# Two routers, a tail and one block's dense part put in a new order, in a kernel of three layers on one core

## The reference

```python
x = x + concat([mla_out, rw_out]) @ w_o
t = rms_norm(x, g_ffn)                       # block 1
group_logits = t @ w_group + b_group         # 4 groups, the best one is taken
expert_logits = t @ w_expert + b_expert      # 8 experts in it, the best two
weights = softmax(top_vals) * group_probs[gsel]
x = x + sum_e combine[:, e] * ((silu(t @ w_gate[e]) * (t @ w_up[e])) @ w_down[e])

for i in (0, 1):                             # block 2
    mix = concat([pool(x @ w_in), conv(x @ w_in)]) @ w_out[i]
    x = layer_norm(ALPHA * x + mix, ln1_g[i], ln1_b[i])
    f = swiglu(x) if i == 0 else moe_swiglu(x, router_w)   # 2816 wide; 8 experts, 3584 wide, best two
    x = layer_norm(ALPHA * x + f, ln2_g[i], ln2_b[i])
    x = x + sigmoid(x @ ple_gate_w[i]) * (p[i] @ ple_w[i])
```

## Time and profile before

| what | value |
|---|---|
| time, median of 3 runs | 1973.67 us (1969.62 to 1973.97) |
| the profiled execution | 1974.57 us |
| its span in the trace | 1972.8 us |
| TensorE busy | 1765.5 us (89%) |
| VectorE busy | 452.2 us (23%) |
| ScalarE busy | 197.6 us (10%) |
| read from memory | 543.5 MB, 276 GB/s over the span |
| granted clock of TensorE, mean | 0.956 of full speed |

### The profile page before, as it was taken

The page is one execution under the profiler, slowest core; times in us unless marked ns, Lnnn a source line. Parts: engine busy times, 40 slices in busy tenths (PEclk is TensorE's granted clock), DMA queues, the critical chain, the costliest instruction groups (busy, mean ns, idle before and its releaser), DMA issues.

```text
span 1972.8 us, 21931 instructions
## 1 busy us (share of the span) xinstructions
PE 1765.5 (89%) x9504; PEld 946.2 (48%) x9504; DVE 452.2 (23%) x771; ACT 197.6 (10%) x333; POOL 41.2 (2%) x123
## 2 busy tenths in 40 slices
PE   7888867677698999989989999999989999998778
PEld 6676654443484444455755434444444434432233
DVE  2664631121273000022832011011011011010003
ACT  2241111111102000001120000000000000000001
POOL 4001000000000000000000000000000000000000
PEclk9889869998899999999988999999999999999999
DMA  7022238999926234353417999979999999999991
GB/s 260 3 86 87 103 117 361 422 422 422 399 93 222 94 128 149 107 200 131 145 50 285 413 386 377 397 301 413 411 406 411 412 414 403 402 409 414 413 403 42
DMA packets 134949, 548.13 MB, mean 278 GB/s; under 512 B 7577, under 2 KB 12802, under 8 KB 107218
## 3 DMA queue, kind: packets, MB, share of 16 engines
q1 hardware_dynamic: 131744, 540.67, 69.6%
q0 software_dynamic: 1664, 5.05, 0.8%
q10 hardware_dynamic: 1458, 1.19, 0.2%
HBM read 543.50 MB, written 1.05 MB: 276 GB/s over the span
## 4 chain that ended last, share of the span: by engine, by line
PE 76%; DMA 10%; DVE 7%; SPq 3%; issue 2%; ACT 2%; DVEq 0%; ACTq 0%
PE ps L1909 15%; PE ps L1916 9%; PE ps L1943 7%; DMA ring<-in_exp_w 5%; DMA ring<-in_w_down 5%; PE ps L1951 4%; PE ps L1792 4%; PE ps L1770 4%; PE ps L1799 4%; PE ps L1665 3%; PE ps L1612 3%; PE ps L1565 2%; PE ps L1548 1%; PE ps L1749 1%; PE ps L1709 1%
## 5 line engine op out<-in xcount | busy, mean ns | idle before, releaser
L1909 PE MATMUL ps<-ring,xT 128*128 128x512 f32 x672 | 292.8, 594 | 3.6 <-DMA ring<-in_exp_w 2.4
L1916 PE MATMUL ps<-ring,xT 128*64 128x512 f32 (+3 forms) x1536 | 226.7, 480 | 17.6 <-DMA ring<-in_exp_w 17.5
L1909 PEld LDWEIGHTS ps<-ring,xT 128*128 128x128 f32 x672 | 126.4, 190 | 164.5 <-issue 160.2
L1916 PEld LDWEIGHTS ps<-ring,xT 128*64 128x64 f32 (+1 forms) x1536 | 86.3, 128 | 149.9 <-issue 113.2
L1943 PE MATMUL ps<-ring,work 128*128 128x512 f32 x336 | 149.1, 595 | 3.2 <-DMA ring<-in_exp_w 3.2
L2741 DVE TENSOR_TENSOR work<-work,ps 128x512 f32<-128x512 f32 (+3 forms) x32 | 38.4, 1201 | 463.1 <-PE ps L1909 302.1
L1951 PE MATMUL ps<-ring,work 128*64 128x512 f32 (+1 forms) x672 | 113.6, 524 | 11.6 <-DMA ring<-in_exp_w 11.6
L1943 PEld LDWEIGHTS ps<-ring,work 128*128 128x128 f32 x336 | 62.0, 190 | 78.4 <-issue 78.4
L1125 ACT ACTIVATE work<-ps 128x512 f32<-128x512 f32 (+3 forms) x32 | 21.2, 661 | 675.7 <-PE ps L1916 353.7
L1612 PE MATMUL ps<-xT,ring 128*128 128x256 f32 x384 | 85.7, 387 | 0.0
L1792 PE MATMUL ps<-ring,xT 128*128 128x512 f32 (+1 forms) x192 | 80.0, 571 | 0.7 <-ACT xT L1025 0.7
(11 more groups left out here) (519 smaller groups left out, 1619.1 us busy)
## 6 DMA issues: line engine op xcount, KB each, us to landing
ring<-in_exp_w SPq DMA_DIRECT2D x168, 2048.0 KB, 15.5
ring<-in_w_up SPq DMA_DIRECT2D x32, 1024.0 KB, 16.5
ring<-in_w_down SPq DMA_DIRECT2D x32, 1024.0 KB, 19.0
ring<-in_w_gate SPq DMA_DIRECT2D x32, 1024.0 KB, 9.6
ring<-in_dense_w SPq DMA_DIRECT2D x15, 2048.0 KB, 7.8
ring<-in_w_in SPq DMA_DIRECT2D x6, 2048.0 KB, 11.8
ring<-in_w_in SPq DMA_DIRECT2D x8, 1104.0 KB, 15.8
ring<-in_w_out SPq DMA_DIRECT2D x4, 2048.0 KB, 14.8
```

What stands on the lines that cost most here:

```text
L1909: ins = mm(ps[:, bank + b, :], slots_k(m, k), w[:, i, b * 512:(b + 1) * 512], start=start, stop=stop)
L1916: ins = mm(ps[n * j:n * (j + 1), bank, 0:c], slots_k(m, k), columns, start=start, stop=stop, tile_position=(0, n * j))
```

## The change

**First router.** `g_ffn` is folded into the router's weights once, early, on GpSimd (`w_both`, groups and experts side by side, 40 columns). x itself is transposed instead of the normed x, tile 0 inside the last `w_o` products of tile 1, and the scale of each token is applied to its logits. So each tile's logits are one group of products. The mask is computed first; the weights and the flag move behind the first quad's selection, on VectorE. The gather waits for the first selection only. Extra products without a reader (`keep_warm`) stand before and after `places`.

**Block 2, layer 0.** The first dense products of tile 0 start when tile 0 is turned; tile 1's transposes follow them, into banks 4 and 5. p is turned during the last dense step, the ple products go to banks 0 to 3, the gate to 4 to 7, and gate, sigmoid, product and sum go by 512 columns.

**Second router.** Logits by tile, extra products after each and after `places`, mask before weights; the gather waits for the first selection; both halves are copied out before the weights are worked out.

**Tail.** The overflow flag is read by TensorE after pair 0. p is turned and copied in the last pair. Also: the first transposes of block 2 wait for the last sums of block 1 (`q_add`) instead of VectorE's set-up (`done`).

```diff
-        wg_sb = cut(rtr, 0, KD, NG)
-        we_sb = cut(rtr, KD * NG, KD, E1)
+        w_both = cut(rtr, 0, KD, 8 + E1)
+        b_both = cut(rtr, KD * (8 + E1), 8 + E1)
...
-            for dst, src in ((wg_sb, w_group[0].rearrange("(p k) n -> p k n", k=KD)),
+            for dst, src in ((w_both[:, :, 0:NG], w_group[0].rearrange("(k p) n -> p k n", p=P)),
+                             (w_both[:, :, 8:8 + E1], w_expert[0].rearrange("(k p) n -> p k n", p=P)),
...
+            pool.wait_ge(ld_rtr, 16 * 5)
+            pool.wait_ge(*dve_f("cols"))
+            pool.tensor_tensor(w_both, w_both, spread(cols[:, ROWS["g_ffn"]:ROWS["g_ffn"] + KD], 2, 8 + E1),
+                               ALU.mult).then_inc(rtr_ready, 1)
...
                 for n in range(2):
+                    if t == 1 and n == 1:
+                        turn_half_tiles(0)
                     for k in range(4):
                         ins = mm(ps[:, 2 * t + n, :], mixT[:, 4 + k, t * P:(t + 1) * P], w_o_b[:, k, n * 512:(n + 1) * 512],
...
+            def keep_warm(n, bank):
+
+                for _ in range(n):
+                    mm(ps[:, bank, 0:2 * P], before[:, :], x_sb[:, 0, 0:2 * P], start=True, stop=True)
...
-            turn_x(xn, m1p, "xT", lambda t: [m1d(f"xn {t}"), dve_f("x1 1")])
-            pe.wait_ge(ld_rtr, 16 * 5)
+            pe.wait_ge(rtr_ready, 1)
+            pe.wait_ge(*m1a("xT 1"))
+            m1p.raise_by(logits(6, 0, 8 + E1, w_both), "logits 0")
+            turn_half_tiles(1)
             pe.wait_ge(*m1d("xT 3"))
-            logits(NG, wg_sb, 0)
-            m1p.raise_by(logits(E1, we_sb, 8), "logits")
+            m1p.raise_by(logits(7, 1, 8 + E1, w_both), "logits 1")
+            keep_warm(8, 2)
             pe.wait_ge(*m1d("mask"))
             places(m1p, E1)
+            keep_warm(2, 2)
...
-                pe.wait_ge(q_sel, it + 1)
+                pe.wait_ge(q_sel_w, it + 1)
...
-                turn_x(x_sb, bp, f"xT mix {l}", lambda t: [m1d("done") if l == 0 else bd(f"x 0 {t}")])
+                turn_x(x_sb, bp, f"xT mix {l}", lambda t: [(q_add, 2 * NQ + t)] if l == 0 else [bd(f"x 0 {t} {n}") for n in range(2)])
...
-            turn_x(x_sb, bp, "xT ffn 0", lambda t: [bd(f"ln1 0 {t}")])
-            pe.wait_ge(*ba("xT ffn 0 3"))
+            turn_tile(x_sb, bp, "xT ffn 0", 0, [bd("ln1 0 0")])
+            pe.wait_ge(*ba("xT ffn 0 1"))
...
+                    if (u, t) == (0, 0):
+                        turn_tile(x_sb, bp, "xT ffn 0", 1, [bd("ln1 0 1")], 4)
...
+                turn_tile(x_sb, bp, "xT ple 0", 0, [bd("ln2 0 0")], 6)
+                pe.wait_ge(*ba("xT ple 0 1"))
+                gate(0, 0)
+                turn_tile(x_sb, bp, "xT ple 0", 1, [bd("ln2 0 1")], 6)
+                gate(0, 1)
+                pe.wait_ge(*ba("xT ple 0 3"))
+                gate(1, 0)
+                gate(1, 1)
...
-            turn_x(x_sb, bp, "xT ffn 1", lambda t: [bd(f"ln1 1 {t}")])
+            turn_tile(x_sb, bp, "xT ffn 1", 0, [bd("ln1 1 0")])
+            pe.wait_ge(*ba("xT ffn 1 1"))
+            logits(4, 0, E2, w_router)
+            keep_warm(6, 3)
+            turn_tile(x_sb, bp, "xT ffn 1", 1, [bd("ln1 1 1")])
             pe.wait_ge(*ba("xT ffn 1 3"))
-            bp.raise_by(logits(E2, w_router, 8), "logits")
+            bp.raise_by(logits(5, 1, E2, w_router), "logits")
+            keep_warm(4, 3)
             pe.wait_ge(*bd("mask"))
             places(bp, E2)
+            keep_warm(2, 3)
...
-            for p in range(PAIRS):
+            pair_pe(0)
+            pe.wait_ge(*bd("over"))
+            extra2 = pe.value_load(over_i[0:1, 0:1], min_val=0, max_val=S // CAP2 - 1)
+            for p in range(1, PAIRS):
                 pair_pe(p)
             for t in range(TT):
                 last_scatter(t)
-            extra2 = pe.value_load(over_i[0:1, 0:1], min_val=0, max_val=S // CAP2 - 1)
...
+            first_sum(0)
+            scale_of(0)
+            normed_rows(0)
+            first_sum(1)
+            group_of(0)
...
+            scale_of(1)
+            group_of(1)
...
+            normed_rows(1)
             dve.wait_ge(*m1p("places"))
-            slots(m1d, E1, CAP1)
+            slots(E1)
...
+                if first:
+                    token_weights()
+                    link(red(over, ps[:, 6, 2 * E1:3 * E1], AX_X, ALU.max))
...
             take_wide(0)
+            take_wide(1)
+            two_weights(bd, ba)
```

More of the change, by code:

```diff
@@ L133 @@
     "moe1_pe": [
-        "xT 0", "xT 1", "xT 2", "xT 3", "logits", "places",
+        "xT 0", "xT 1", "logits 0", "xT 2", "xT 3", "logits 1", "places",
     ],
     "moe1_act": [
-        "squares 0", "squares 1", "std", "exp",
+        "squares 0", "std 0", "xT 0", "xT 1", "squares 1", "std 1", "exp",
     ],
     "moe1_dve": [
-        "var", "xn 0", "xn 1", "xT 0", "xT 1", "xT 2", "xT 3", "diffs", "mask", "over", "done",
+        "var 0", "xn 0", "xT 2", "xT 3", "var 1", "mask", "xn 1", "diffs", "over", "done",
     ],
@@ L2418, in _, with first_sum @@
             mixed_rows(1)
-            for t in range(TT):
+            m1a, m1d, m1p = m1["act"], m1["dve"], m1["pe"]
+            ba, bd, bp = bl["act"], bl["dve"], bl["pe"]
+            def first_sum(t):
                 dve.wait_ge(*pe_f(f"w_o {t}"))
```

278 lines of the change are left out of this document (153 added, 125 removed), and 12 rows, old and new, of the table STEPS.

## The result

The changed kernel takes 1924.61 us (median of 4 runs, 1923.22 to 1926.11) against 1973.82 us before; the ratio is 0.9755, with a 95% interval of 0.9733 to 0.9776. Measured again it was 0.9749 (0.9721 to 0.9777); two of the six runs of that second measurement, 7752 us and 1972 us (the latter at a mean clock of 0.928), were slow ones and are left out of it. The forecast was 1929.2. The profiled execution took 1926.11 us with a span of 1924.4, so the two spans differ by 48.4 us where the sum had 45.4.

What follows compares the result with a forecast made beforehand. Transfers bound the 32-expert and later pair stages, TensorE the dense part; the edit shortens gaps between. 22.0 + 0 + 3.3 + 9.4 + 5.0 + 5.7 = 45.4 us off 1974.57 gives 1929.2 us (1923 to 1936).

Steps and rivals of the forecast that it cites:

- Part 1: First router, up to the first expert product: 22.0 us gained (16.6 cold to 26.4 with the clock up).
- Part 2: Entry of block 2, transposes no longer waiting for VectorE's set-up: 0 us gained (0 to 3.4).
- Part 3: Dense part beginning with tile 0, ahead of tile 1's transposes: 3.3 us gained (2.4 to 4.2).
- Part 4: Gate of layer 0, ple products directly behind the dense part: 9.4 us gained (7.0 to 10.5).
- Part 5: Second router, up to the pair products: 5.0 us gained (-3.4 to 9.4).
- Part 6: Tail, from the last scatter through the ple products: 5.7 us gained (1.5 to 7.1).
- (a): Both routers and tail: added products don't raise the clock in time; gain 27.4 us, 1947.2 us in all; chance 0.15.
- (b): Routers, dense part, gate and tail: the clock never falls; gain 54.2 us, 1920.4 us in all; chance 0.17.
- (c): Tail: jump is the gap, ple products no earlier and cold; layer 0 gate gains 7.0; 1935.8 us; chance 0.10.
- (d): Pair stage short of transfers from its start, second router gains only 1.6 us; 1932.6 us in all; chance 0.06.
- (e): Early weight loads: router weights in many short runs hold up first weights by 16 us or more; slower; chance 0.03.
- (f): First router: weight-load time depends on columns alone, not clock; loses 0 to 1.8 us, 1931.0 us; chance 0.02.

Runs made afterwards that it cites:

- first trace: First profiled execution of the changed kernel, nothing further changed: 1926.11 us, span 1924.4.
- second trace: Profiled execution of the changed kernel run once more, same code: 1916.35 us, span 1914.6; median 1920.07 us.
- the filled kernels: Changed kernel with added products in TensorE's gaps: 1916.94 us; also ahead of w_o: 1912.71 us, again 1909.63; four more front gaps: 1904.06 us.

## Why the prediction was right, point by point

- **Where the time is and that it adds up: right.** The 32-expert stage passed its start on to 0.2 us, and the pair stage did too but for 1.4 us. That 1.4 is within what the stage differs by from one execution to the next: 876.17 in one trace of the changed kernel and 874.21 in the other (994.02 to 1868.23), 874.75 before.
- **Part 1, right in kind, short by 2.4 us.** The step that failed is "I take them cold, 3.5 us" for the logits of tile 1: they took 1.98, the clock was still up. The eight products then ended 5.2 us later and not 6.2. These two are the 2.4. That is so in ten of the twelve traces with one run of logits a tile; in the two others they took 3.63, as forecast, and where the stretch can be compared it was 20.4 us instead of 18.98. In three it was 17.7 to 17.8, near the warm bound of the part. So the step had no fixed value, and the sum took one. The kernel with the logits apart shows that passes with few columns cost more than their time, 5.9 to 8.6 us for 3.5 us of them at the full clock. A reading was off too: the 43.32 us for 192 passes, taken as warm, began at a clock of 0.67 (536 to 541 us); warm they are 41.64, 0.217 us a pass and not 0.226, which changes the sum by less than 0.2.
- **Part 2, right for the transposes; the stretch moved for another reason.** The transposes gained nothing, 4.15 us behind the last sum before and 4.19 after. The 1.6 us of the table are another pause, 1.46 us in the short products behind the transposes, gone in this trace, back in two others (1.16 and 1.13 us), and 2.36 and 2.70 us in two whose first pause was missing. In the run without the blocks none of the pauses is left, so they belong to the jump as far as one trace shows it.
- **Part 3, right:** 3.0 us (2.6 and 0.4 of transposes of p), against 3.3; the start was 4.3 earlier and 0.4 colder. The run that undoes it gives 2.7, and 3.4 with the first groups taken as equally warm.
- **Part 4, right:** 6.5 against 6.4 to the gate products, 1.0 against 1.1 in them, 2.7 against 1.9 behind them. The missed 0.8 is the clock: the transposes and short products ahead of the mixer run warm now, and so does the start of the mixer itself, 41.64 us for the 192 passes that take 43.32 us cold at the start. The sum had left out this after-effect, 1.3 us, and the same in layer 0, 1.4.
- **Part 5, right in six traces of eight.** 5.4 against 5.0 in the first trace, by the steps of the forecast: tile 0's logits cold (3.45 against 3.5), the six products 4.51 against 5.4 since the clock rose within them, all behind them warm. In the second trace and in one other the clock rose only behind them, and the gain was 3.0. "The price of the edit" is real: six products in front of ready transposes take 4.5 to 5.3 us, and without any added product the router is no slower than the worse of the two traces. The bounds (-3.4 to 9.4) were the honest part of this step.
- **Part 6, right in kind, 0.9 us too much in the first trace, 2.4 in the second.** "I take 2.0 us of the 3.26" failed: 2.81 stayed, because only the reading of the flag (0.5) had moved and the jump had not. The other step, "then 7.0 warm", held in the first trace by luck: the products were warm in three traces of eleven (7.10) and took 8.6 to 8.8 in the others. The usual gain is the 3.3 of the second trace, not 4.8.
- **The rivals.** (a), the products don't raise the clock in time, holds for the second router in two of eight traces. (b), the clock never falls, is what happened in the first router up to 263 us in the first trace and all through in the second, and what the filled kernels show in both routers and at the dense start; its 1920.4 was for a state that the changed kernel has in parts. (c), the jump is the gap, was right about the cause and about the products behind it in eight traces of eleven, though not in the first; part 4 did not fall to its low end, as (c) had it. (d) did not happen: the pair stage passed the gain on. (e) did not show: with the same router-weight loads the first group of w_o started between 230.5 and 238.2 us, on both sides of the 234.59 of before. (f) was set on the wrong side: where both halves of the logits together cost 3.5 us, the sum, which has 1.8 and 3.5, would gain 1.8 and not lose it. They took 1.73 and 1.98, which a warm clock gives as well; the passes of 0.22 us in the run with the logits apart speak against (f).
- **The single numbers** came out closer than the method deserved. The sum missed the spans' difference by 3.0 us in the first trace and by 12.8 in the second, whose span is 1914.6. From one execution to another of the same code its single terms differ by 2.7 (first router), 2.8 (dense), 2.5 (second router), 1.6 (tail) and 6.6 us (front).

## What to carry to other kernels

Fill TensorE's dependent waits, not its queue: a few products that write a free bank, placed right in front of a wait and short enough to end with it, cost nothing, and the groups in the table above were at the full clock behind them in every trace here. With some 60 of them in all the gaps the kernel took 1904 us instead of 1925. The same products in front of ready work cost their own 4.5 us or more: 20.4 to 22.8 us in the second router with them, 22.2 without. Cost passes with few columns at both levels of the clock, 0.11 and 0.22 us each here, and say which level the sum takes and why. And before a term of a sum is checked against a trace, look at a second trace of the same kernel: the terms above differ by 1.6 to 2.8 us, and the front part by 6.6, with no cause in the code.

## What the hardware showed that I had not expected

- TensorE busy without a pause from 256.8 to 263.8 us with passes of 8 and 32 columns stayed at 1.2 GHz in the run with the logits apart, and fell to it from 2.4 GHz during such passes (the clock was 1.00 up to 253 us and 0.50 from 254 us on).
- A block of code that is only skipped costs 6.9 us at the entry of block 2 and 3.0 us at the tail, against the first trace. The pause isn't fixed: from the last sum to the first mixer product the same program took 10.0 us in one execution and 4.8 in another (501.96 to 511.95, 496.44 to 501.19), in the second with the pause of 2.36 us in the middle of short products:

```profile
498.22 2.36 issue
```

- The same program, in the same ten microseconds of its front part, ran at either level of the clock; over the thirteen traces with this place unfilled, w_o started 3.8 us earlier on average at the full one (four traces against nine).
